# Block 2 scores from split q and k: two float32r passes for two float32 ones, rotation in place, an earlier query column

## The reference, cut to what matters

```python
q, k = rms_norm(q, q_g), rms_norm(k, k_g)
q, k = axial_rope(q, ang), axial_rope(k, ang)             # kinds A and C
logits = jnp.einsum("bqhgd,bkhd->bhgqk", qb, k).astype(jnp.float32) * scale
p = jax.nn.softmax(logits, axis=-1)
```

## Time and profile before

| what | us |
|---|---|
| median of 3 runs | 2466.03 |
| lowest, highest of them | 2460.39, 2472.28 |
| the profiled execution, its own time | 2468.51 |
| its span, first to last instruction | 2466.4 |
| TensorE busy in it | 2223.9 (90%) |
| VectorE, ScalarE, GpSimd busy | 1314.5 (53%), 1033.0 (42%), 912.5 (37%) |
| columns of layer 0 (A), first score to first score | 28.2 each |
| of layer 1 (B) | 27.65 |
| of layer 2 (C) | 26.2 to 27.8 |
| of layer 3 (A without context queries) | 17.2 |

### The profile page before, as it was taken

The page is one execution under the profiler, slowest core; times in us unless marked ns, Lnnn a source line. Parts: engine busy times, 40 slices in busy tenths (PEclk is TensorE's granted clock), DMA queues, the critical chain, the costliest instruction groups (busy, mean ns, idle before and its releaser), DMA issues.

```text
span 2466.4 us, 39608 instructions
## 1 busy us (share of the span) xinstructions
PE 2223.9 (90%) x14736; PEld 1854.9 (75%) x14736; DVE 1314.5 (53%) x2688; ACT 1033.0 (42%) x1978; POOL 912.5 (37%) x588
## 2 busy tenths in 40 slices
PE   6969899998788998899999898999889899888898
PEld 5868899987788998667766876776778566666677
DVE  4594556547844664356651235556224766723565
ACT  4433466453435654533322244332334445425332
POOL 0444378005453840333422133332313434333443
PEclk8989999989899999899979999999989899888898
DMA  6423556653345655311122321112232111223121
GB/s 220 146 85 107 187 174 193 188 171 113 103 128 172 196 189 188 120 35 44 41 88 68 120 86 56 61 52 73 86 106 92 52 43 35 79 76 120 52 69 52
DMA packets 72848, 262.92 MB, mean 107 GB/s; under 512 B 8032, under 2 KB 10208, under 8 KB 72416
## 3 DMA queue, kind: packets, MB, share of 16 engines
q1 hardware_dynamic: 71392, 256.31, 32.5%
q0 software_dynamic: 1280, 4.20, 0.6%
HBM read 259.43 MB, written 1.05 MB: 106 GB/s over the span
## 4 chain that ended last, share of the span: by engine, by line
PE 65%; DVE 18%; issue 6%; ACT 6%; POOL 5%; DMA 0%; DVEq 0%; ACTq 0%; SPq 0%; POOLq 0%
PE gemm L421 13%; PE gemm L422 12%; PE gemm L423 12%; PE gemm L688 6%; PE score L727 5%; DVE r L1348 3%; PE obank L759 3%; PE tbank L657 3%; DVE d L1294 2%; PE stat L668 1%; PE obank L763 1%; POOL arena L1830 1%; POOL w_lo L294 1%; DVE zt L1256 1%; DVE small L1554 1%
## 5 line engine op out<-in xcount | busy, mean ns | idle before, releaser
L294 POOL TENSOR_TENSOR w_lo<-ring,w_hi 128x1024 fp32r<-128x1024 f32 x252 | 605.6, 2408 | 556.0 <-ACT w_hi L874 554.7
L421 PE MATMUL gemm<-g_hi,w_hi 128*128 128x256 f32 x1344 | 395.2, 294 | 42.3 <-POOL w_lo L294 28.1
L421 PE MATMUL gemm<-h_hi,w_hi 128*128 128x512 f32 (+1 forms) x928 | 388.5, 419 | 12.4 <-DVE h_lo L1635 9.6
L874 ACT ACTIVATE w_hi<-ring 128x1024 fp32r<-128x1024 f32 x344 | 361.7, 1053 | 81.3 <-PE gemm L423 39.9
L422 PE MATMUL gemm<-g_lo,w_hi 128*128 128x256 f32 x1344 | 383.9, 286 | 0.0
L423 PE MATMUL gemm<-g_hi,w_lo 128*128 128x256 f32 x1344 | 383.8, 286 | 0.0
L422 PE MATMUL gemm<-h_lo,w_hi 128*128 128x512 f32 (+1 forms) x928 | 353.1, 381 | 0.0
L423 PE MATMUL gemm<-h_hi,w_lo 128*128 128x512 f32 (+1 forms) x928 | 352.8, 380 | 0.0
L421 PEld LDWEIGHTS gemm<-g_hi,w_hi 128*128 128x128 f32 x1344 | 264.7, 197 | 62.2 <-POOL w_lo L294 36.2
L1189 ACT ACTIVATE pr<-score,small 128x512 f32<-128x512 f32 (+1 forms) x192 | 128.0, 669 | 392.8 <-DVE small L1556 390.5
L421 PEld LDWEIGHTS gemm<-h_hi,w_hi 128*128 128x128 f32 x928 | 180.5, 195 | 148.4 <-issue 108.2
(11 more groups left out here) (278 smaller groups left out, 3885.4 us busy)
## 6 DMA issues: line engine op xcount, KB each, us to landing
ring<-wall SPq DMA_DIRECT2D x478, 512.0 KB, 3.7
r<-nbias POOLq DMA_DIRECT2D x16, 256.0 KB, 3.0
cst<-consts SPq DMA_DIRECT2D x1, 2340.5 KB, 10.3
r<-x_t SPq DMA_DIRECT2D x1, 1024.0 KB, 4.7
x<-ctx_t SPq DMA_DIRECT2D x1, 1024.0 KB, 15.5
y_t<-x SPq DMA_DIRECT2D x4, 256.0 KB, 2.3
d<-pos SPq DMA_DIRECT2D x1, 128.0 KB, 10.2
```

The costliest lines, as they stand in the source:

```text
L294: eng.tensor_tensor(w_lo[:, q % SPLITS, :, :], ring[:, t % RING, :, :], w_hi[:, q % SPLITS, :, :].bitcast(F), ALU.subtract)\
L421: pe.matmul(out, w[0][:, k, :], x[0], start=start, stop=False)
L874: act.activation(w_hi[:, q % SPLITS, :, :], ring[:, t % RING, :, :], ACT.Copy).then_inc(S["hi_ready"], 1)
```

## The change

It does four things.

1. `q_both` holds for each head the query's high part (float32r) on the head's own 64 partitions and its low part on the other 64; `k_high` holds the key's high part on both halves of the partitions (`k_twice`, in kind B `k_twice_even` and `k_twice_odd`), `k_low` the key's low part. A score tile is one float32r pass over 128 rows, (q high and q low) by k high, and one over 64 rows, q high by k low.
2. The parts have to be made. ScalarE: `k_split_high`, 4 copies of 64x512 for a key chunk, and `q_split_high`, 2 for a query column. VectorE: `q_split_low`, 2 differences of 64 rows, last in a column. GpSimd: `k_split_low`, 2 differences of 64x512 for a key chunk. Kind A does both of its first key chunks at the layer's start (chunk c // 4 is used), B and C do chunk c+1 in column c.
3. The rotation of the query works in `raw` itself; `raw` is given back after `q_split_low`.
4. `evac_q` of the next column is after unit NU // 2 - 1; `q_sums` and `q_start` are in the unit after, `q_end`, `q_rms` and `q_split_high` two after (at most NU - 1).

```diff
+        q_both = nc.alloc_sbuf_tensor_at("q_both", [P, 2, 2, N2], FR, offset=d1_at)
+        k_twice = nc.alloc_sbuf_tensor_at("k_twice", [P, 2, 2, N2], FR, offset=r1_at)
+        k_low = nc.alloc_sbuf_tensor_at("k_low", [P, KC, N2], FR, offset=arena_at + 4 * 8192)
...
+        def q_evac_at(NU):
+            return NU // 2 - 1
...
                     if u == 0:
-                        pe.wait_ge(S["roped"], rbase(L) + nk + c + 1)
+                        pe.wait_ge(S["q_split"], L * KC + c + 1)
+                        pe.wait_ge(S["k_split"], kbase(L) + (nk if kind == "A" else c + 1))
...
-                    if t < 2:
-                        ins = pe.matmul(bk[:, :], q[:, t * P:(t + 1) * P], kT[a:a + HD, kc, :], start=True, stop=True)
...
+                    for tile_, to, at, w in ((t, 0, 0, N2),) if t < 2 else ((2, 0, T, C), (3, C, T, C)):
+                        pe.matmul(bk[:, to:to + w], q[:, tile_ * P:(tile_ + 1) * P], kh[:, at:at + w], start=True, stop=False)
+                        ins = pe.matmul(bk[:, to:to + w], q[a:a + HD, tile_ * P:(tile_ + 1) * P], kl[:, at:at + w], start=False, stop=True)
...
-                        if u == NU - 2 and c + 1 < KC:
+                        if u == q_evac_at(NU) + 1 and c + 1 < KC:
                             q_sums(c + 1)
...
+                def k_split_high(j):
+                    for hh in range(2):
+                        a = HD * hh
+                        for to in (0, HD):
+                            ins = act.activation(k_high(kind, j, hh)[to:to + HD, :], kT[a:a + HD, j, :], ACT.Copy)
+                    ins.then_inc(S["k_hi_ready"], 1)
+
+                def q_split_high(c):
+                    R = rbase(L) + nk + c
+                    if kind != "B":
+                        act.wait_ge(S["roped"], R + 1)
+                    for hh in range(2):
+                        a = HD * hh
+                        ins = act.activation(q_both[a:a + HD, c % 2, hh, 0:NQ], raw[a:a + HD, R % 2, 0:NQ], ACT.Copy)
+                    ins.then_inc(S["q_hi_ready"], 1)
...
                 act.wait_ge(S["roped"], rbase(L) + nk)
+                for j in range(2 if kind == "A" else 1):
+                    k_split_high(j)
+                if kind != "B":
+                    q_split_high(0)
                 evac_z(0)
...
-                        if u == NU // 2 and c + 1 < KC:
+                        if u == 1 and kind != "A" and c + 1 < KC:
+                            k_split_high(c + 1)
+                        if u == min(q_evac_at(NU) + 2, NU - 1) and kind != "B" and c + 1 < KC:
+                            q_split_high(c + 1)
+                        if u == q_evac_at(NU) and c + 1 < KC:
                             evac_q(c + 1)
...
+                def q_split_low(c):
+                    R = rbase(L) + nk + c
+                    dve.wait_ge(S["q_hi_ready"], L * KC + c + 1)
+                    for hh in range(2):
+                        a, to = HD * hh, HD * (1 - hh)
+                        ins = dve.tensor_tensor(q_both[to:to + HD, c % 2, hh, 0:NQ], raw[a:a + HD, R % 2, 0:NQ],
+                                                q_both[a:a + HD, c % 2, hh, 0:NQ].bitcast(F), ALU.subtract)
...
+                    dve.sem_inc(S["q_split"], 1)
+                    dve.sem_inc(S["raw_used"], 1)
...
                         biggest(c, u)
-                        if u == NU - 1 and c + 1 < KC:
+                        if u == min(q_evac_at(NU) + 2, NU - 1) and c + 1 < KC:
                             q_end(c + 1)
...
-                        if u == NU - 2 and c + 1 < KC:
+                        if u == q_evac_at(NU) + 1 and c + 1 < KC:
                             q_start(c + 1)
+                        if u == min(q_evac_at(NU) + 2, NU - 1) and c + 1 < KC:
+                            q_rms(c + 1)
                         if u == NU - 1 and c + 1 < KC:
-                            q_rms(c + 1)
+                            q_split_low(c + 1)
...
+                def k_split_low(j):
+                    pool.wait_ge(slot_used[n["split"] % RING], n["split"] // RING + 1)
+                    pool.wait_ge(S["k_hi_ready"], kbase(L) + j + 1)
+                    for hh in range(2):
+                        a = HD * hh
+                        seq(pool.tensor_tensor(k_low[a:a + HD, j, :], kT[a:a + HD, j, :], k_high(kind, j, hh)[a:a + HD, :].bitcast(F), ALU.subtract))
+                    pool.sem_inc(S["k_split"], 1)
+
                 q_side(0)
+                for j in range(2 if kind == "A" else 1):
+                    k_split_low(j)
                 q_pow(0)
...
                     if c + 1 < KC:
+                        if kind != "A":
+                            k_split_low(c + 1)
                         q_side(c + 1)
                         q_pow(c + 1)
```

More of the change, by code:

```diff
@@ L291, in lo_parts @@
                 if PLAN[t] == who:
+                    state["split"] = t
                     q = int(SPLIT_NO[t])
@@ L304, in units, with k_high @@
             return [(t, hh) for hh in range(2) for t in tiles]
+        def k_high(kind, kc, hh):
+            if kind == "B":
+                return (k_twice_odd if kc % 2 else k_twice_even)[:, hh, :]
+            return k_twice[:, kc % 2, hh, :]
+        def q_evac_at(NU):
+            return NU // 2 - 1
         def lag(kind):
@@ L1124, in block2 @@
                         rk(j - 1)
+                def k_split_high(j):
[12 more added lines that the diff above has]
+                    ins.then_inc(S["q_hi_ready"], 1)
                 def evac_q(c):
                     evac_qk(rbase(L) + nk + c, sq[:, 2 + c % 2, 0:NQ], cc(f"qg{L}"), S["q_sq"], NQ)
+                    if kind == "B":
+                        q_split_high(c)
                 def evac_z(c):
@@ L1638, in block2 @@
                 q_end(0)
+                q_split_low(0)
                 q_rms(0)
```

44 lines of the change are left out of this document (27 added, 17 removed).

## The result

The changed kernel takes 2586.39 us (median of 4 runs, 2582.78 to 2591.0); the kernel before took 2463.21 us beside it. The ratio is 1.0495, 95% interval 1.046 to 1.053: slower by 5%, more than twice what was forecast. The profiled execution has a span of 2585.3 us against 2466.4, 118.9 us more.

What follows compares the result with a forecast made beforehand. TensorE was taken as the bound in layers 0, 1 and 3. Layers 0 to 3 -8, +13, +30, +13, starts +18, ends -12: +54 on 2468.5, so 2522, as a median 2520 us; range 2446 to 2552.

Steps and rivals of the forecast that it cites:

- Part 1: Scores on TensorE: a unit falls from 1.05 to about 0.47 us, 102 us of TensorE in all.
- dear passes: Rival on score passes: they don't get cheaper than 0.34 us; at most 2545 us; chance 0.03.
- Part 2: Column ends, layers 0 and 1: the first score waits for VectorE's differences; columns 26.3 (-1.9) and 28.9 us (+1.25).
- layer 0's race: Layer 0's column end: VectorE's second difference starts 0.2 us ahead of GpSimd's `w_lo`; column 26.3 us, 28.7 if GpSimd wins.
- The port: GpSimd's `w_lo` and, in layers 1 to 3, its power block VectorE's `rope_end` or differences until they end.
- Part 3: Layer 2: copies and GpSimd's splits delay the query; column 31.6 us, +4.3 each, +30 in all.
- Part 4: Layer 3: blocked `rope_end` and differences end the column at 18.3 against 17.2 us, +1.1; TensorE waits 4 us.
- Part 5: Clock: new gaps in layers 0, 1 and 3 cost 0.75 us in each of 21 columns, +16.
- the clock falls in every column: Rival on the clock: 28 columns lose 1.55 us instead of 21 at 0.75, +27, 2547 us; chance 0.12.
- Part 6: Layer starts and ends: key splits at starts +18 (layer 0 +5.3), last columns' cheaper scores -12.
- the unblocked case: Rival on VectorE's port: differences and `rope_end` are not blocked; sum -26, 2440 us; chance 0.15.

Runs made afterwards that it cites:

- the two experiments: Changed kernel with the score's second pass over 128 rows, 2501.04 us; changed kernel with context units' passes ordered high, low, low, high, 2572.06 us.
- cheap passes: Second score pass over 128 rows: in the changed kernel 2501.04 us; with the query's differences also ahead of the output (layer 2's 29.3 us column) 2450.74 us.
- the run in layer 3: Changed kernel with GpSimd's `w_lo` after the sine product moved behind the power in layer 3: 2584.32 us, ratio 1.0486.
- both edits: Changed kernel with the second score pass over 128 rows and the query's differences ahead of the output: 2450.74 us, ratio 0.9937.

## Why the prediction was wrong

The sign was right, and so were the places of the waits save in part of layer 2; the size was not: 2520 forecast, 2586 measured, outside the range.

- **Part 1, the step that failed most.** "A unit's score falls from 1.05 to about 0.47 us." It is 0.84, and 1.23 for a context unit. I took both passes from runs of like passes, though the second has 64 rows and no row had float32r at 64, and I bounded it by 0.34; the two steps are 0.41 and 0.43. Four units at 0.37 more and two at 0.76 more are 3.0 us a column in layers 0 to 2, and 0.10 for the projection pass behind each unit comes on top; taking the rows' change away gave 85 us, for in layer 1 half of the wait went as well. The Trainium skill (TensorEngine Tiling (Array Packing), Key Properties) says that changing the tiling mode drains TensorE. The loads in the changed kernel and in the two experiments agree. It should have stood in the prediction as the rule against this change; I had costed only "dear passes" at 0.34 and a chance of 0.03.
- **Part 2, layer 0's race.** I had the second difference ahead of `w_lo` by 0.2 us; `w_lo` came with the first. From the end of unit 5's maximum to `w_lo` I counted 3.3 us; in the trace it is 1185.10 to 1187.44, 2.3. The dear passes have a part in it: the second difference comes 0.70 us too late, with cheap passes 0.15. So 0.35 us of the error is the race's own, and a forecast lead of 0.2 us was too thin to choose a side by. The price of losing it, 2.4 us a column, was named; the side taken was wrong.
- **The port.** Right for `w_lo` in every layer, and shown by the run in layer 3. Wrong for the power: in layer 2 the differences take 0.70 each while it runs (1.66 us from 2133.60). In layer 1 the `w_lo` behind the power holds the second difference, as in layer 0, and the column came to 32.3 against 28.9 without the clock's share. The Trainium skill (SBUF — State Buffer, Who interferes with whom) has the pair held for the whole instruction; the rows of `w_lo` agree, those of the power don't.
- **Part 3, layer 2.** +26 against +30, by the chain as written, and shown to come with the splits (26.5 us a column without them, 29.3 with them and cheap passes). The total agrees partly by luck. The last six columns take 31.9 us each, against the 31.6 forecast for all; the first takes 23.3. And errors cancelled: scores 3.0 us dearer, mostly inside waits, a clock down from 0.94 to 0.87, for which nothing was charged here, and no block by the power.
- **Part 4, layer 3.** +15 against +13 is luck. The last six columns grow by 3.2 us each where 1.85 was forecast (1.1 and the clock's 0.75), and the first shrinks by 4.1, which no part of the prediction has and no run explains. The wait of 0.68 for the sums went, and TensorE's wait is 3.0 where I had 4; but TensorE is busy for 17.6 us where I counted 14.2: four scores at 0.37 more, and the clock at 0.87.
- **Part 5, the clock.** I charged 0.75 us to each of 21 columns. It is about 2 in layer 0, and every column has its spell. The rival "the clock falls in every column" was the better part of the truth, at 1.55; its 2547 us fell short since scores and race were missing from it.
- **Part 6.** The first score of layer 0 comes 5.7 us later (5.3 forecast), and TensorE's wait before it grows from 5.23 to 11.21; how near the first figure is means little, for with the same start the other runs have that score between 1057.0 and 1064.5 us. The stretches from a layer's last column to the next layer's first score, and from layer 3's to the end, are longer by 4.3, 4.7, 3.4 and -0.1 us; with the first that is 18 against my 6. These hold a start and an end each, which no run took apart; but with cheap passes the four together are longer by 3.5 us instead of 12.3, so most of the miss is that the scores of the last columns didn't get cheaper.

So of the 65 us missed, layer 0 makes 38 (race, scores, clock), layer 1 17, ends 12, layer 3 2, and layer 2 gives 4 back. The range had a slip of its own, without weight here: its lower end, 2446, is called the unblocked case, whose sum is 2440.

## What to carry to other kernels

A float32r pass is cheap only among passes with the same number of rows; before splitting a product into passes, look at the tile of each in the trace and count the changes, and fill the rows up rather than change them, where the surplus product is harmless. Put the last producer of the next column's input into the slot where its engine waits for TensorE anyway, not behind what TensorE does last: the wait costs its length and a spell at the half clock on top. And a split pays only where the engine that makes it has time: here, against float32 scores at the same places, it gained 3 and 4 us a column in two layers and lost 3 and 1 in the other two, so it belongs in the first two alone.

## What the runs showed of the hardware

- A change of rows (128 to 64 or back) between neighbouring float32r passes leaves the next weight load (0.18 to 0.19 us) bare in both directions; without a change the load starts beside the running pass. The pass behind a change is 0.10 us late as well (0.33 instead of 0.23 at 512 columns, 0.22 instead of 0.12 at 256).
- The first 128-row pass of 512 columns behind the 64-wide value passes takes 0.32 us to the next, its followers 0.23. With the second pass at 128 rows, its weights load at 1121.39, only 0.03 us ahead of it, as behind a change; whether that is the cause wasn't tried.
- GpSimd's power over 8 columns (1.66 us) doesn't hold up VectorE's two-operand instruction, which takes 0.70 us beside it; its 1024-column difference does, to 0.54 us past its own end. Where VectorE's starts 0.01 us ahead, it keeps its 0.69 us, and GpSimd's difference takes 2.88 us instead of 2.38.
- After 3.92 us without a matmul TensorE ran its next 5.98 us at 0.50, the lower of its two levels, 1.2 GHz; after waits of 0.49 us in the same place it stayed at 1.00, and so it did after 1.05 and 1.29 us with both edits.
